# A blocked triangular inverse on TensorE: the second of three tile groups writes to the opposite partitions and is interleaved with the first

## What is computed

```python
def gdn_block(S, q, k, v, g, beta):          # one chunk, L = 64
    ...
    a_mat = jnp.where(strict, bt[..., :, None] * kk * dec, 0.0) + jnp.eye(L)
    rhs = jnp.concatenate([v * bt, k * bt * exp(G)], axis=-1)
    sol = lax.linalg.triangular_solve(a_mat, rhs, left_side=True, lower=True)
    u = sol[..., :A_DV] - sol[..., A_DV:] @ S
    ...
```

## Time and profile before

| | us |
|---|---|
| median of 3 runs (lowest, highest) | 3338.81 (3337.06, 3345.41) |
| the profiled execution | 3340.13 |
| its span | 3338.4 |
| TensorE busy in the span | 3257.5 (98%) |
| VectorE, ScalarE, GpSimd busy | 1433.4, 1097.6, 437.7 |

### The profile page before, as it was taken

How to read it: one execution, slowest core, us unless ns; L and a number is a source line. 1 busy time by engine, 2 the same in 40 slices (tenths; PEclk the granted TensorE clock), 3 DMA queues, 4 the chain that set the end, 5 groups by cost and what they waited for, 6 DMA issues and landing times. The chain is left out here.

```text
span 3338.4 us, 50225 instructions
## 1 busy us (share of the span) xinstructions
PE 3257.5 (98%) x17973; PEld 2517.6 (75%) x17973; DVE 1433.4 (43%) x3584; ACT 1097.6 (33%) x2854; POOL 437.7 (13%) x509
## 2 busy tenths in 40 slices
PE   7999999999899999999999998999999999999999
PEld 4677777776588888888777675888888888777676
DVE  2455555555355555555443234243343243343233
ACT  3433333333144444444210343133333233210341
POOL 1433344433000000000001002000000000011000
PEclk8999999999999999999999999999999999999999
DMA  5211111213321111112461102111111101461101
GB/s 156 72 45 33 40 31 44 38 45 93 102 59 41 39 49 49 47 32 45 148 202 57 38 1 72 46 38 48 52 55 43 55 25 55 151 207 57 38 1 53
DMA packets 255336, 208.88 MB, mean 63 GB/s; under 512 B 29616, under 2 KB 232272, under 8 KB 255144
## 3 DMA queue, kind: packets, MB, share of 16 engines
q1 hardware_dynamic: 249790, 196.65, 20.5%
q10 hardware_dynamic: 5360, 9.67, 0.8%
HBM read 160.30 MB, written 45.99 MB: 62 GB/s over the span
## 5 line engine op out<-in xcount | busy, mean ns | idle before, releaser
L525 PE MATMUL gdn_pj<-hT,Wb 128*128 128x352 f32 x1536 | 525.4, 468 | 15.7 <-ACT gdn_zraw L764 14.1
L525 PEld LDWEIGHTS gdn_pj<-hT,Wb 128*128 128x128 f32 x1536 | 266.3, 192 | 110.8 <-ACT gdn_zraw L764 14.7
L2103 PE MATMUL gla_pj<-gla_TX,gla_S 128*128 128x256 f32 (+1 forms) x736 | 191.2, 393 | 0.0
L2103 PE MATMUL gla_pj<-hT,gla_S 128*128 128x256 f32 (+1 forms) x736 | 187.1, 393 | 0.0
L1794 ACT ACTIVATE band_E<-band_NS,band_nm 128x576 f32<-128x576 f32 (+9 forms) x136 | 89.8, 660 | 213.5 <-DVE band_nm L1924 213.2
L2103 PEld LDWEIGHTS gla_pj<-hT,gla_S 128*128 128x128 f32 x736 | 139.4, 190 | 26.2
L2103 PEld LDWEIGHTS gla_pj<-gla_TX,gla_S 128*128 128x128 f32 x736 | 138.2, 190 | 26.2
L2103 PE MATMUL band_pj<-hT,Wb 128*128 128x256 f32 x512 | 136.2, 387 | 9.0 <-PEq L45 7.6
L2103 PE MATMUL band_pj<-hT,band_S 128*128 128x288 f32 (+1 forms) x512 | 143.1, 397 | 0.0
L2103 PE MATMUL band_pj<-band_TX,band_S 128*128 128x288 f32 (+1 forms) x512 | 140.6, 395 | 0.0
L1657 PEld LDWEIGHTS band_PX<-band_ET,band_VT 128*128 128x128 f32 x976 | 128.7, 191 | 12.4 <-issue 1.7
(11 more groups left out here) (535 smaller groups left out, 6347.4 us busy)
## 6 DMA issues: line engine op xcount, KB each, us to landing
Wb<-in_l_w_in_dram SPq DMA_DIRECT2D x95, 512.0 KB, 7.9
fin_xT<-x_features SPq DMA_DIRECT2D x16, 528.0 KB, 7.2
fin_R<-o_features SPq DMA_DIRECT2D x16, 528.0 KB, 9.9
Wb<-in_l_w_mkv_dram SPq DMA_DIRECT2D x8, 1024.0 KB, 5.4
Wb<-in_l_w_out_dram SPq DMA_DIRECT2D x16, 512.0 KB, 4.2
o_features<-gla_OF ACTq DMA_DIRECT2D x14, 528.0 KB, 7.5
gla_Wv<-in_l_w_in_dram SPq DMA_DIRECT2D x7, 1024.0 KB, 5.5
gdn_GB<-gate_rows SPq DMA_DIRECT2D x8, 544.0 KB, 3.7
```

The source lines that it names most:

```text
L525: mm = pe.matmul(pj[:, m % 2, 0:w], W[:, j, k, :], hT[:, k, c0:c0 + w], start=k == 0, stop=k == KD - 1)
L2103: mm = pe.matmul(bank[:, 0:w], left(name, k), right(name, k, unit[0], w), start=name in ("P1", "P5", "P2") and k == 0, stop=k == FAST_K - ...
```

## The change

A helper `crossed(g)` pairs each half P that a matmul reads with the half Q that it writes: P itself for groups 0 and 2, the opposite half for group 1. TensorE first waits for groups 0 and 1 together, then issues their twelve matmuls tile by tile, alternating between the groups; group 2 follows with its own waits. ScalarE's copy and VectorE's subtraction of group 1 have to bring the halves back, so each becomes two instructions of 64 partitions; at l = 5 VectorE already had two.

```diff
+        def crossed(g):
+            return [(P, HALVES[1 - a if g == 1 else a]) for a, P in enumerate(HALVES)]
...
                     for l in range(1, LEVELS):
-                        for g in range(3):
-                            pe.wait_ge(masked, h * 18 + 3 * l + g + 1)
-                            pe.wait_ge(tm_ok, h * 15 + 3 * (l - 1) + g + 1)
+                        for two in ((0, 1), (2,)):
+                            for g in two:
+                                pe.wait_ge(masked, h * 18 + 3 * l + g + 1)
+                                pe.wait_ge(tm_ok, h * 15 + 3 * (l - 1) + g + 1)
                             for t in range(3):
-                                for P in HALVES:
-                                    mm = pe.matmul(P3[P, g, ...], BT[P, ...], TM[P, ...], ...)
-                            mm.then_inc(v_done, 1)
+                                for g in two:
+                                    for P, Q in crossed(g):
+                                        mm = pe.matmul(P3[Q, g, ...], BT[P, ...], TM[P, ...], ...)
+                                    if t == 2:
+                                        mm.then_inc(v_done, 1)
                         fill(1)
...                      (the X block in the same way: v_out, vb_ok and tail_out of groups 0 and 1
...                       ahead of their matmuls, X3[Q, g, ...] written, x_done when t == 2)
                         fill(FILL["level"] - 1)
...
-                            act.activation(own(VV, g), p3_own(P3, g), ACT.Copy).then_inc(v_out, 1)
+                            if g == 1:
+                                for P, Q in crossed(g):
+                                    v = act.activation(own(VV, g)[P, :, :], p3_own(P3, g)[Q, :, :], ACT.Copy)
+                            else:
+                                v = act.activation(own(VV, g), p3_own(P3, g), ACT.Copy)
+                            v.then_inc(v_out, 1)
...
                             if l < LAST:
-                                dve.tensor_tensor(g3(TI, g), g3(TI, g), p3_own(X3, g), ALU.subtract).then_inc(tt_ok, 1)
+                                if g == 1:
+                                    for P, Q in crossed(g):
+                                        mm = dve.tensor_tensor(g3(TI, g)[P, :, :], g3(TI, g)[P, :, :], p3_own(X3, g)[Q, :, :], ALU.subtract)
+                                else:
+                                    mm = dve.tensor_tensor(g3(TI, g), g3(TI, g), p3_own(X3, g), ALU.subtract)
+                                mm.then_inc(tt_ok, 1)
                                 dve.wait_ge(tt_ok, h * 18 + 3 * l + g + 1)
                                 dve.transpose(own(TM, g), g3(TI, g)).then_inc(tm_ok, 1)
                             else:
-                                for P in HALVES:
-                                    mm = dve.tensor_tensor(g3(TT, g)[P, :, P], ..., p3_own(X3, g)[P, :, :], ALU.subtract)
+                                for P, Q in crossed(g):
+                                    mm = dve.tensor_tensor(g3(TT, g)[P, :, P], ..., p3_own(X3, g)[Q, :, :], ALU.subtract)
```

More of the change, by code:

```diff
@@ L621, in head @@
                     for l in range(1, LEVELS):
-                        for g in range(3):
-                            pe.wait_ge(masked, h * 18 + 3 * l + g + 1)
-                            pe.wait_ge(tm_ok, h * 15 + 3 * (l - 1) + g + 1)
+                        for two in ((0, 1), (2,)):
+                            for g in two:
+                                pe.wait_ge(masked, h * 18 + 3 * l + g + 1)
+                                pe.wait_ge(tm_ok, h * 15 + 3 * (l - 1) + g + 1)
                             for t in range(3):
-                                for P in HALVES:
-                                    mm = pe.matmul(P3[P, g, 64 * t:64 * t + 64], BT[P, 3 * g + t, 0:64], TM[P, 3 * g + t, 0:64],
-                                                   start=True, stop=True)
-                            mm.then_inc(v_done, 1)
@@ L630, in head @@
-                        fill(1)
[L631 to L636, removed]
-                            for t in range(3):
-                                for P in HALVES:
-                                    mm = pe.matmul(X3[P, g, 64 * t:64 * t + 64], VV[P, 3 * g + t, 0:64], TI[P, 3 * g + t, :],
-                                                   start=True, stop=True)
-                            mm.then_inc(x_done, 1)
+                                for g in two:
+                                    for P, Q in crossed(g):
+                                        mm = pe.matmul(P3[Q, g, 64 * t:64 * t + 64], BT[P, 3 * g + t, 0:64], TM[P, 3 * g + t, 0:64],
+                                                       start=True, stop=True)
+                                    if t == 2:
+                                        mm.then_inc(v_done, 1)
@@ new lines, in head @@
+                        fill(1)
+                        for two in ((0, 1), (2,)):
+                            for g in two:
+                                pe.wait_ge(v_out, h * 15 + 3 * (l - 1) + g + 1)
+                                if l == 1:
+                                    pe.wait_ge(vb_ok, h * 3 + g + 1)
+                                    if g == 2:
+                                        pe.wait_ge(tail_out, h + 1)
+                            for t in range(3):
+                                for g in two:
+                                    for P, Q in crossed(g):
+                                        mm = pe.matmul(X3[Q, g, 64 * t:64 * t + 64], VV[P, 3 * g + t, 0:64], TI[P, 3 * g + t, :],
+                                                       start=True, stop=True)
+                                    if t == 2:
+                                        mm.then_inc(x_done, 1)
@@ L1034, in head @@
                             else:
-                                for P in HALVES:
-                                    mm = dve.tensor_tensor(g3(TT, g)[P, :, P], g3(TI, g)[P, :, :], p3_own(X3, g)[P, :, :], ALU.subtract)
+                                for P, Q in crossed(g):
+                                    mm = dve.tensor_tensor(g3(TT, g)[P, :, P], g3(TI, g)[P, :, :], p3_own(X3, g)[Q, :, :], ALU.subtract)
                                 mm.then_inc(tt_ok, 1)
```

## The result

The changed kernel takes 3348.31 us (median of 10 runs, 3343.85 to 3349.97); the kernel before, timed beside it, takes 3340.61 (10 runs, 3337.06 to 3348.66). The ratio is 1.0019, with an interval of 1.001 to 1.0028: 6 to 8 us slower, where the forecast was 4.6 us faster. The profiled execution took 3348.97 us, its span 3347.3 us.

A forecast was written before the change was run, and what follows sets the result against it. TensorE bounds the kernel, busy 92.96 of a head's 93.30 us. Gains of 0.71 us a head, 5.0 in seven heads, less 0.4 in the last, make 4.6: 3338.8 to 3334.2 us; own range 3331 to 3337, wide range 3328 to 3350.

The forecast's parts named there:

- What the array gives: TensorE's X and V blocks: four quarters work at once, 24 records in the time of 12, 0.35 us less a block.
- Rival 2: TensorE issues no faster than two quarters' rate, so groups 0 and 1 take 0.70 us together: 3353.7 us, chance 0.24.
- X to V: X block to next level's V block, levels 1 to 4, heads 0 to 6: 2.57 us against 2.58, gain counted as 0.
- last head: Head with shorter steps: VectorE's 2.57 us against 2.25 loses 0.32 four times; -0.38 us in sum.
- V to X, levels 2 to 5: V block to X block within a level: 1.94 us against 1.99, gain 0.05 in each of four levels.
- The first V and X: Level 1 of a head: V starts 0.13 us late, X follows at 1.69, gain 0.16 us.
- The last X: Last X block of a head, where VectorE already has two halves: the 0.35 us gain is kept whole.
- Rival 1: VectorE's halves are cheap, unheld behind the transpose and 0.35 us apart: 4.5 us more gain, 3329.7 us, chance 0.20.
- Rival 3: A head's gain is swallowed by a wait taken to move along, such as ahead of line 599: 3339 us, chance 0.06.

The follow-up runs named there:

- straight_late: `after_late` with group 1 writing to its own partitions, interleaved order, halves and waits kept: 3352.82 us in one execution.
- after_late: The kernel after, with SyncE holding the next head's four weight loads until the running head's last X block is done: 3342.03 us, ratio 0.9997 to the kernel before.
- after_again: The kernel after measured once more without an edit: 3348.9 us, ratio 1.0021 to the kernel before.
- v_only: The kernel before with only the V block crossed and interleaved, ScalarE's copy of group 1 in halves: 3332.63 us, ratio 0.997.

## Why the prediction was wrong, step by step

**What the array gives** was right. Of group 0 and 1 thirteen records start in 0.20 us, four in each 58.5 ns, and blocks that wait for nobody are 0.35 us shorter. `straight_late` shows that the quarters do it. Rival 2, the rate of two quarters, falls, and with it the price worked out from the Trainium skill ("TensorE: Matmul & The Clock Gate", section "Wait — 56ns, not 53.3ns?"), which has starts never less than about 25 ns apart. Four starts in 58.5 ns are 14.6 ns each on average, so the measurement decides against it here.

**X to V** was right in its mechanism: 0.35 us of the X block turned into a wait for VectorE. My steps stand within 0.02 us up to the transpose's end: transpose of group 0 at 0.99 us behind X (1.01 forecast), the halves at 1.40 (1.40) and 0.36 to 0.37 apart, group 1's transpose at 2.16 (2.14), its end at 2.54 (2.52). The failed term is the last, "0.05 later TensorE starts". I took it from a place where one wait is tied to a load; here `tm_ok` is waited for in an instruction of its own, and V's first matmul starts 0.145 us behind the end. V comes at 2.68 or 2.69, where the sum had it unchanged at 2.58, in four places a head: 0.44 us. The merged loop puts four waits in a row ahead of V's first matmul, and the prediction gave none of them a price of its own. In the last head it is 2.69 against 2.25, a loss of 0.44 where I had 0.32.

**V to X, levels 2 to 5**: 1.94 forecast and measured. ScalarE's halves take the time of a full copy each (0.66 for two), as priced.

**The first V and X**: V starts 0.24 us late, not 0.13. X follows at 1.875, not 1.69: it waits for group 1's copies (end 713.61) and starts its loads at 713.84, 0.23 behind them, again with waits of their own ahead of the load. X is 0.13 late instead of 0.16 early: 0.29 us a head. **The last X** gave its 0.35.

A head thus came out at 93.33 to 93.43 us where it has no gap, not 92.6: the 0.71 of gain are used up by 0.44 + 0.29, most of it for the release behind separate waits, and the 5.0 us of gain in seven heads became a loss of a few tenths. The last head lost 0.9, not 0.4. Had this been all, the time would have been about 1 us over before's. `after_late` fits that: 3342.03, no difference that can be measured.

**What the sum did not have at all** is the late instruction packet, 6 to 7 us, nearly all of the measured difference. This is the step that turned no change into a loss: the sum priced matmuls, copies and releases, and put the supply of TensorE's instructions at nothing without a reason. I argued that the rest of a head runs at TensorE's pace and that its one wait moves along. But instructions are fetched too, and the fetch stands in a DMA queue beside the loads. I read the granted clock, the waits and the five engines, and neither the queues of the page nor the load at 617 us. Even with them I could not have computed the gap: before, the packet of head 5 came at 618.22, in the last moment ahead of the load's data. Why it did not come ahead of the load in the kernel after, no run shows. What could have been written is a rival: one packet that misses its slot costs the rest of an 8.8 us load, less what TensorE still has in hand. Here that was a gap of 3.6 us and the lower clock behind it.

**The rivals.** Rival 1 (cheap halves) falls: 0.36 to 0.37 apart and held behind the transpose. Rival 3 had the right outcome for a head, a gain swallowed, by another mechanism than its own: not a wait that moves along, but the release of each block. That 3348.31 lies within 3328 to 3350 is luck: the upper end came from rival 2, and no rival had the mechanism that made the kernel slower.

## What to carry to other kernels

Where a block is on the path and another engine follows on its heels, shorten only the side whose follower has slack: here the crossed V block brought 0.35 us a level and the crossed X block, which splits an instruction on VectorE, brought nothing. When several waits are merged ahead of one matmul, count each as an instruction: tied to a load it cost 0.05 us here, on its own 0.115, and with another behind it 0.27. Read the instruction queue against the large loads; if a gap in the middle of a block is put down to "issue", look for the packet that ends it and move the load.

## What the runs showed of the hardware

Three things I had not expected. TensorE can stand still for want of instructions: in five gaps (packets ending at 250.49 and 627.15 in the kernel after, at 251.00 and 629.43 in `after_again`, at 618.73 in `v_only`) work goes on 1.25 to 1.46 us behind the end of a 16 KB packet, and in head 5 the packet came each time as the last data of a 512 KB load passed. Such a gap can also cost clock: in the kernel after the granted clock was 0.50 from 627.24 to 634.06, and four 352-column records took 2.71 us instead of 1.45. And four 64 x 64 quarters work at once even where two of them share their rows and two their columns, here in different banks: four starts in 58.5 ns, the same 58.5 ns in which two quarters make two.
